# A mixture-of-experts stage: order of the turns, the gather and the scatter on the matmul engine

## The reference

```
def hierarchical_moe(h, ...):            # 512 tokens, 32 experts in 4 groups, 2 experts per token
    g_idx = top group of each token; top_i = top 2 experts of that group
    gates = p_g * softmax(top_v)
    for each expert e, over its tokens:
        y = (silu(xb @ w1[e]) * (xb @ w3[e])) @ w2[e]     # 1024 -> 512 -> 1024
    x += sum over the chosen experts of gate * y
return rms_norm(x, final_norm_g)
```

## Time and profile before

| | us |
|---|---|
| median of 3 runs | 3057.76 (3057.33 to 3059.06) |
| span of the profiled execution | 3050.7 |
| PE busy in the span | 2915.5 (96%) |
| DVE, ACT, POOL busy in the span | 1497.9, 1060.0, 1081.4 |
| first gather of the experts' stage starts at | 2512.8 |
| first turn starts at | 2537.9 |
| last scatter starts at | 3031.8 |

### The profile page before, as it was taken

The page is one execution under the profiler, slowest core; times in us unless marked ns, Lnnn a source line. Parts: engine busy times, 40 slices in busy tenths (PEclk is TensorE's granted clock), DMA queues, the critical chain, the costliest instruction groups (busy, mean ns, idle before and its releaser), DMA issues. The chain is left out here.

```text
span 3050.7 us, 48369 instructions
## 1 busy us (share of the span) xinstructions
PE 2915.5 (96%) x20376; PEld 2203.6 (72%) x20377; DVE 1497.9 (49%) x1866; ACT 1060.0 (35%) x1540; POOL 1081.4 (35%) x623
## 2 busy tenths in 40 slices
PE   8998999999999899899999999999988989999997
PEld 6777878888888777787888888877757754444543
DVE  5287423468862528742436887258864231222223
ACT  5553243343332345324334333254454331111112
POOL 4263134444444336412444444433434220010000
PEclk9999999999999999999999999999999989999999
DMA  4120022222222322102222222222123147999995
GB/s 167 66 83 23 4 87 104 85 93 99 98 105 90 110 70 80 36 4 75 96 92 97 97 97 99 95 94 70 56 69 101 55 180 307 399 398 399 398 374 232
DMA packets 55792, 402.73 MB, mean 132 GB/s; under 512 B 7840, under 2 KB 8992, under 8 KB 15648
## 3 DMA queue, kind: packets, MB, share of 16 engines
q1 hardware_dynamic: 55584, 399.77, 34.6%
HBM read 397.65 MB, written 2.10 MB: 131 GB/s over the span
## 5 line engine op out<-in xcount | busy, mean ns | idle before, releaser
L1157 POOL TENSOR_TENSOR back_w_lo<-w,back_w_hi 128x1024 fp32r<-128x1024 f32 (+1 forms) x240 | 541.8, 2266 | 638.2 <-ACT back_w_hi L1317 638.0
L1317 ACT CAST back_w_hi<-w 128x1024 fp32r<-128x1024 f32 (+1 forms) x240 | 229.8, 957 | 511.6 <-PE bank L1173 503.1
L1168 PE MATMUL bank<-h_hi,back_w_hi 128*128 128x512 f32 x1072 | 268.4, 392 | 1.5 <-DVE back_made_lo L1498 1.5
L1170 PE MATMUL bank<-h_lo,back_w_hi 128*128 128x512 f32 x1072 | 264.8, 389 | 0.0
L1173 PE MATMUL bank<-h_hi,back_w_lo 128*128 128x512 f32 x1072 | 264.7, 389 | 0.0
L261 POOL TENSOR_TENSOR front_w_lo<-w,front_w_hi 128x1024 fp32r<-128x1024 f32 x68 | 178.0, 2620 | 243.7 <-ACT front_w_hi L445 243.7
L1168 PEld LDWEIGHTS bank<-h_hi,back_w_hi 128*128 128x128 f32 x1072 | 201.1, 188 | 47.3 <-issue 3.8
L3085 PE MATMUL bank<-moe_w,moe_hg 128*64 128x512 f32 x1024 | 232.5, 597 | 0.0
L1170 PEld LDWEIGHTS bank<-h_lo,back_w_hi 128*128 128x128 f32 x1072 | 201.2, 188 | 41.8
L1173 PEld LDWEIGHTS bank<-h_hi,back_w_lo 128*128 128x128 f32 x1072 | 201.2, 188 | 41.8
L1893 POOL TENSOR_TENSOR mid_w_lo<-w,mid_w_hi 128x1024 fp32r<-128x1024 f32 x62 | 151.3, 2443 | 212.9 <-ACT mid_w_hi L2353 212.6
(11 more groups left out here) (589 smaller groups left out, 5834.3 us busy)
## 6 DMA issues: line engine op xcount, KB each, us to landing
moe_w<-in_moe_w SPq DMA_DIRECT2D x128, 1024.0 KB, 11.5
moe_w<-in_moe_w SPq DMA_DIRECT2D x32, 2048.0 KB, 11.7
w<-in_ffn_up SPq DMA_DIRECT2D x44, 1024.0 KB, 4.8
w<-in_w_merge SPq DMA_DIRECT2D x22, 1536.0 KB, 6.5
w<-in_w_in SPq DMA_DIRECT2D x30, 1024.0 KB, 4.8
w<-in_w_mid SPq DMA_DIRECT2D x29, 1024.0 KB, 4.8
w<-in_ffn_down SPq DMA_DIRECT2D x16, 1408.0 KB, 5.9
w<-in_w_out SPq DMA_DIRECT2D x16, 512.0 KB, 4.0
```

The costliest lines, as they stand in the source:

```text
L1157: nc.gpsimd.tensor_tensor(split(B.w_lo, n), raw(n), split(B.w_hi, n).bitcast(F32), ALU.subtract).then_inc(f["w_lo"], 1)
L1168: nc.tensor.matmul(bank, B.w_hi[:, n % 2, k, :], x_hi[:, cols], start=start and k == 0, stop=False)
L1170: nc.tensor.matmul(bank, B.w_hi[:, n % 2, k, :], x_lo[:, cols], start=False, stop=False)
L1317: nc.scalar.copy(split(B.w_hi, n), raw(n)).then_inc(f["w_hi"], 1)
```

## The change

- The four transposes of the middle activations come ahead of those of the selection, and ACT copies them in that order.
- The gather and the gate sums of the next quad come behind both turns and ahead of the down matmuls. As banks 4 and 5 now serve the scatter too, the gather first waits for the adds of tiles 4 and 5. ACT's copies of the gather come behind its copies of the turns.
- The scatter uses banks 4 to 7 in two visits a pair of four tiles each: after `k` = 2 of `up`, and behind `up`. The first visit also waits until ACT has taken the gate sums out of bank 4. The credit of `added` is 4.
- DVE adds tiles 0 to 3 ahead of `mid` and tiles 4 to 7 behind it.

The core of the diff:

```diff
-        up_banks, y_banks, hg_banks, add_banks = T.ps[0:2], T.ps[2:4], T.ps[4:6], T.ps[6:8]
+        up_banks, y_banks, hg_banks, add_banks = T.ps[0:2], T.ps[2:4], T.ps[4:6], T.ps[4:8]
...
             def scatter(g, k):
 
                 pe.wait_ge(sems["added"], KD * g + k + 1)
-                nc.tensor.matmul(add_banks[k % 2][:, :], y_hi[:, k * P:k * P + P], selT[:, :], start=True, stop=False)
-                nc.tensor.matmul(add_banks[k % 2][:, :], y_lo[:, k * P:k * P + P], selT[:, :], start=False,
+                bank = add_banks[k % 4]
+                nc.tensor.matmul(bank[:, :], y_hi[:, k * P:k * P + P], selT[:, :], start=True, stop=False)
+                nc.tensor.matmul(bank[:, :], y_lo[:, k * P:k * P + P], selT[:, :], start=False,
                                  stop=True).then_inc(sems["scattered"], 1)
...
-            def turn_and_down(g, s, b):
-
-                for m in range(4):
-                    mm = nc.tensor.transpose(y_banks[1][:, m * P:m * P + P],
-                                             sel[:, s, m, W2 * b:W2 * b + W2].bitcast(F32), T.ident[:, :])
-                mm.then_inc(sems["selT_done"], 1)
+            def turn(g, s, b):
+
                 pe.wait_ge(sems["made"], g + 1)
                 for f in range(4):
                     mm = nc.tensor.transpose(up_banks[0][:, f * P:f * P + P], mid[:, f * P:f * P + P],
                                              T.ident[:, :])
                 mm.then_inc(sems["mid_turned"], 1)
+                for m in range(4):
+                    mm = nc.tensor.transpose(y_banks[1][:, m * P:m * P + P],
+                                             sel[:, s, m, W2 * b:W2 * b + W2].bitcast(F32), T.ident[:, :])
+                mm.then_inc(sems["selT_done"], 1)
+
+            def down(g):
+
                 pe.wait_ge(sems["midT_taken"], g + 1)
...
                     g = 2 * q + b
+                    turn(g, s, b)
                     if b == 1 and more:
+                        pe.wait_ge(sems["added"], KD * g + 2)
                         gather(q + 1, 1 - s)
                         sum_gates(q + 1, 1 - s)
-                    turn_and_down(g, s, b)
+                    down(g)
 
                     def step(k):
                         if k == 2:
                             pe.wait_ge(sems["y_lo"], 2 * g + 2)
-                        if k in (2, 4, 6):
-                            scatter(g, k - 2)
-                            scatter(g, k - 1)
+                            pe.wait_ge(sems["gates_taken"], q + 1 + b)
+                            for tile in range(4):
+                                scatter(g, tile)
 
                     if b == 0 or more:
                         pe.wait_ge(sems["hg_act"], 2 * q + 2 * b + 3)
                         pe.wait_ge(sems["hg_dve"], 2 * q + 2 * b + 3)
                         up(g + 1, 1 - b, step)
-                        scatter(g, 6)
-                        scatter(g, 7)
+                        for tile in range(4, KD):
+                            scatter(g, tile)
...
@@ ACT's program @@
+                    act.wait_ge(sems["mid_turned"], g + 1)
+                    nc.scalar.copy(flat(midT[:, :, :]), up_banks[0][:, :]).then_inc(sems["midT_taken"], 1)
+                    act.wait_ge(sems["selT_done"], g + 1)
+                    nc.scalar.copy(selT[:, :], y_banks[1][:, :]).then_inc(sems["selT_taken"], 1)
                     if b == 1 and more:
                         rows(q + 1, 0)
                         rows(q + 1, 2)
                         take_gates(q + 1, 1 - s)
-                    act.wait_ge(sems["selT_done"], g + 1)
-                    nc.scalar.copy(selT[:, :], y_banks[1][:, :]).then_inc(sems["selT_taken"], 1)
-                    act.wait_ge(sems["mid_turned"], g + 1)
-                    nc.scalar.copy(flat(midT[:, :, :]), up_banks[0][:, :]).then_inc(sems["midT_taken"], 1)
...
@@ DVE's program @@
-                        for k in range(6):
+                        for k in range(4):
                             add(g, k)
                         if b == 0:
                             gated(g + 1, s, 1)
                         else:
                             gated(g + 1, 1 - s, 0)
-                        add(g, 6)
-                        add(g, 7)
+                        for k in range(4, KD):
+                            add(g, k)
```

More of the change, by code:

```diff
@@ L3103, in scatter_last @@
                 if k >= len(last_banks):
-                    pe.wait_ge(sems["added"], KD * g + k - len(last_banks) + 3)
+                    pe.wait_ge(sems["added"], KD * g + k - len(last_banks) + 5)
                 bank = last_banks[k % len(last_banks)]
@@ L3116, in scatter_and_sum @@
             def scatter_and_sum(g):
-                pe.wait_ge(sems["added"], KD * g + 2)
+                pe.wait_ge(sems["added"], KD * g + 4)
                 pe.wait_ge(sems["gates_taken"], quads)
@@ L3153, in _ @@
             for name, credit in (("hg_act", 1), ("hg_dve", 1), ("up_half", 1), ("up_done", 1), ("down_done", 2),
-                                 ("added", 2)):
+                                 ("added", 4)):
                 pe.sem_inc(sems[name], credit)
@@ L3233, in _ @@
                         for k in range(KD):
-                            act.wait_ge(sems["added"], KD * g + k + 3)
+                            act.wait_ge(sems["added"], KD * g + k + 5)
                             if k >= 4:
@@ L3260, in add @@
                 dve.wait_ge(sems["scattered"], KD * g + k + 1)
-                nc.vector.tensor_tensor(T.xT[:, k, :], T.xT[:, k, :], add_banks[k % 2][:, :],
+                nc.vector.tensor_tensor(T.xT[:, k, :], T.xT[:, k, :], add_banks[k % 4][:, :],
                                         ALU.add).then_inc(sems["added"], 1)
```

## The result

The changed kernel takes 3029.85 us (3026.62 to 3030.51) against 3058.41 us (3057.33 to 3061.92) of the kernel before: 0.9903 of it, with a 95% interval of 0.9891 to 0.9914.

What follows compares the result with a forecast made beforehand. PE's own stream was taken to set the time, transfers close behind. Visits −24.0, plain turns +2.6 and turns with a gather +0.7 made −20.7 us, so 3057.8 became 3037.1, range 3033 to 3047.

Steps and rivals of the forecast that it cites:

- Fewer visits: In `up`, to the last visit's first scatter matmul: two visits fewer a pair at 0.33 us; 1.60 us less, 15 times.
- The plain turn: Even pairs and the last, last visit's first scatter matmul to down: 3.05 us becomes 3.37, 0.32 more, 8 times.
- the turn with a gather: Odd pairs but the last, last visit's first scatter matmul to down: 0.04 us more, taken as 0.10, 7 times.
- rival 1: Ahead of the gather: its new wait for DVE's adds replaces the removed stall, losing 5.7 us, giving 3042.8; chance 0.06.
- The first turn: Very first turn of the experts' stage: gains nothing, as it waits for `mid` in either order.
- SP: Weight transfers: none added or dropped; 412 GB/s and 61.1 us of flow a quad, beside 61.2 for PE; pause nearly gone.
- The base: Whole execution: the 7.06 us outside the span stay, so 20.7 us come off the median of 3057.8.
- Rival 4: Behind the plain turns: PE's clock falls to the lower level, losing 40 us, giving 3077; chance 0.04.

Runs made afterwards that it cites:

- `visits_only`: The changed kernel with the two turns, the gather and ACT's copies in the order of before, keeping four banks and two visits a pair: 3052.39 us, ratio 0.9975.
- `turns_only`: The kernel before with the new order of turns and gather alone, keeping two banks and four visits a pair: 3050.05 us, ratio 0.9971.
- `light_pe`: The changed kernel without the y_lo matmuls in the scatter (all pairs but the last) and the h_lo ones in the gather: 3010.75 us, ratio 0.9847.
- the last version: The changed kernel with tile 7 between the two turns at plain turns, and the selection turned first at the stage's first turn: 3027.21 us, ratio 0.9908.

## Why the prediction was right, and where it failed

**Fewer visits: right, a little small.** 1.60 a pair was forecast, 1.69 measured, as the price of a visit is at the upper bound of its range: 0.36 by the added visit, 0.375 by half of 17.71 − 16.02 − 0.94. It isn't one constant, though: for the single visit that stays ahead of V it is 16.02 − 13.90 − 8 × 0.235 = 0.24. 15 × 1.69 = 25.4.

**The plain turn and the turn with a gather: right.** 3.32 against 3.37 and 11.82 against 11.81. The gather's wait costs nothing that the trace lists; rival 1 didn't come.

**The first turn: wrong.** I wrote that it gains nothing because the selection's turn was hidden in the wait. It was, but it also kept that wait short: PE idled 2.38 us behind it, and idles 2.97 without it. This costs 1.0 us by the clock in both traces of the changed kernel.

With these, −15 × 1.69 + 8 × 0.27 + 7 × 0.10 + 1.0 = −21.5, and the undisturbed stages differ by 21.4. The sum of −20.7 was nearly right for this.

**SP: the pause went, as forecast, but the bound was put too near.** I took 412 GB/s and 61.1 us a quad for the flow; that was an average over a stretch with gaps between requests. The flow holds 424, and the bound is 59.3.

**The base: this is the step that failed.** The sum for the stage holds, but "the 7.06 us outside it stay" joined the span of one execution to the median of others. Only 1.8 us lie outside; the other 5 were inside, as the profiled execution was a short one of its kind. The sum was then right for that kind of execution, and I carried it to a median that mostly isn't. In the kernel before, long executions have three low stretches of the clock in the experts' stage, 4.9 us together, and the change removes the gap that stood ahead of them. So the sum lacked a term of −4.9, which the prediction put at nothing. 21.4 + 4.9 = 26.3 is what the stages give for such an execution. The medians differ by 28.6 and 26.7 on two chips. The 0.4 to 2.3 us in between may be the part ahead of the stage, which varies by some 6 us over the traces; that was not settled.

**Rival 4 had the mechanism and the wrong sign.** I priced a fall of the clock as a danger of the change. "The clock is 1.00 through both quads with gaps of 0.75 to 0.81 at every turn" was read as proof that the kernel before is free of it, from two quads of one execution. It is not: at some turns with a gather its clock falls. In small the rival did come, at the first turn, where its price is the 1.0 us above. The rule of the Trainium skill that I cited against the change ("TensorE: Matmul & The Clock Gate", A second HAM failure mode: psum-queue depth-cycling), that brief idle times make the clock swing, agrees with the traces in that the clock falls behind an idle time of 0.81 us. But the number of banks doesn't decide it: `visits_only` has four banks and two such stretches, `turns_only` has two banks and none. What goes with the swing is the gap behind the gate sums. Of the six traces with that gap three have low stretches in the quads. Of the seven others none has, with `light_pe` and its waits for weights left aside. So here the rule spoke for the change, not against it.

What is shown and what is argued: that long executions of before have the stretches, what they cost, and what PE did before them, is in the traces. That they are in most executions is argued, from the medians and from the 47 times above 3054.5; of five traces two have them. That the changed kernel is free of them is read from two traces, and one of the five times of the last version, 3035.33, is 8 us above its median with no trace to say why.

## What to carry to other kernels

Two edits that each look like a gain may only pay together: the merged visits gave matmuls enough to cover the wait for `mid`, and the new order took those matmuls off the way to the gather. Alone they were worth 4.5 and 0.6 us of 21.4, so for each edit work out what becomes late next before you add up. Take the time outside the span from the same execution, and before you trust a clock of 1.00, look at several executions. A gap of the matmul engine can cost more than its length, and it does so only in some of them.

## What the runs showed of the hardware that was not expected

- An idle stretch of 0.81 us of PE behind 32 two-column matmuls and eight transposes was followed by 3.4 us at half the clock in some executions, at every second such turn, +1.69 us each. A stall of 1.19 us ahead of 128 matmuls of 256 columns was not, seven times in one trace.
- Gaps of one length can be hit or spared in one execution: at waits of 2.15 to 2.18 us ahead of the same 24 matmuls the clock fell at one and stayed at 1.00 at two.
- Behind an idle time of 2.97 us at the first turn the clock fell in all seven traces that have it, and the down behind it took 7.59 to 9.17 us; behind one of 2.38 or 2.39 us with four transposes ahead it never fell, in seven traces.
- A further stay in the 128-column form between matmuls of the 64-column form costs 0.36 us beside its matmuls.
- The transfers held 424 GB/s through whole quads, while a printed share of 1.00 also stood beside 411.
- The stage repeats to 0.1 us in undisturbed executions on several chips, while the part ahead of it moves by 6 us.
